# Gated linear attention and the choice of keys in one stage, the bias by distance made at x's load, norms inside the stages that take them

## What is computed

```python
def first_block(x, ...):
    h = rmsnorm(x, norm_g)                                   # n1
    p = h @ w_in                                             # split in gq, gk, gv, gz, ggate, dq, ... pu, pgate
    glog = log_sigmoid(gz @ gate_w2 + gate_b) / 16
    o_gla = rmsnorm(gla_mixer(gq, gk, gv, glog), gla_norm_g) # chunks of 64, state S carried, S = 0 at first
    y_gla = o_gla * silu(ggate)
    score = relu(q_idx . k_idx) weighed over 4 heads; idx = top_k(score, 128)    # the choice of keys
    o_dsa = softmax(q k^T * dh**-0.5 + rel_bias[bucket(t - s)]) v over the chosen keys
    y_dsa = o_dsa * silu(dgate)
    y_pool = ((windowed sums of pu) / count - pu) @ pool_w * pool_scale * silu(pgate)
    return rmsnorm(x + concat(y_gla, y_dsa, y_pool) @ w_out, final_norm_g)       # n2

def _layer_norm(x, gain, bias):                              # n3 to n8; n9 to n12 are rmsnorms
    xf = x - mean(x); return xf * rsqrt(mean(xf * xf) + 1e-5) * gain + bias
```

## Time and profile before

| | |
|---|---|
| three runs | 4337.07, 4345.38, 4340.18 us; median 4340.18 |
| the profiled execution | 4341.67 us, span 4339.9 us |
| TensorE busy, mean granted clock | 3704.6 us (85%), .903 |
| VectorE, ScalarE, GpSimd busy | 1404.9, 694.1, 228.7 us |
| gla stage, select stage, attend stage, pool stage | 299.2 to 418.8, 418.9 to 503.1, 503.2 to 643.7, 643.7 to 659.4 us |
| experts (bound by their loads) | 1476 to 2680 us |

### The profile page before, as it was taken

The page is one execution under the profiler, slowest core; times in us unless marked ns, Lnnn a source line. Parts: engine busy times, 40 slices in busy tenths (PEclk is TensorE's granted clock), DMA queues, the critical chain, the costliest instruction groups (busy, mean ns, idle before and its releaser), DMA issues. The chain is left out here.

```text
span 4339.9 us, 32097 instructions
## 1 busy us (share of the span) xinstructions
PE 3704.6 (85%) x11618; PEld 1792.0 (41%) x11618; DVE 1404.9 (32%) x2445; ACT 694.1 (16%) x1294; POOL 228.7 (5%) x241
## 2 busy tenths in 40 slices
PE   6985787899878499999999998694599767889998
PEld 2534343344343243434343443243344567434444
DVE  0005641177133221121211112427643489611011
ACT  1011120101111111010100000313243233110000
POOL 0000000300000100000000001000000345000000
PEclk8985578999999699999999998796799888999999
DMA  2210761722113599999999996111322000212120
GB/s 67 80 64 2 258 209 58 255 99 78 58 49 153 196 395 398 408 401 408 398 408 399 409 399 231 66 39 61 100 78 78 5 6 1 97 59 78 68 73 34
DMA packets 219295, 729.49 MB, mean 168 GB/s; under 512 B 16207, under 2 KB 27104, under 8 KB 184374
## 3 DMA queue, kind: packets, MB, share of 16 engines
q1 hardware_dynamic: 179132, 629.94, 38.4%
q10 hardware_dynamic: 28394, 55.66, 3.6%
q0 software_dynamic: 11664, 42.47, 2.8%
HBM read 678.33 MB, written 49.69 MB: 168 GB/s over the span
## 5 line engine op out<-in xcount | busy, mean ns | idle before, releaser
L1621 PE MATMUL bank<-moe_gu,all_hT 128*128 128x512 f32 x1088 | 472.1, 595 | 0.0
L1120 PE MATMUL bank<-all_hT,early_w 128*128 128x512 f32 x896 | 390.0, 598 | 22.6 <-PEq L135 11.7
L1811 DVE TENSOR_TENSOR all_hT<-bank,moe_bias 128x512 f32<-128x512 f32 x51 | 35.3, 691 | 973.6 <-PE bank L1621 683.3
L1621 PEld LDWEIGHTS bank<-moe_gu,all_hT 128*128 128x128 f32 x1088 | 207.6, 191 | 261.3 <-issue 261.3
L1647 PE MATMUL bank<-moe_dn,moe_rows 128*128 128x512 f32 x544 | 264.3, 648 | 46.2 <-DMA moe_dn<-in_w_dn_dram 45.3
L1120 PEld LDWEIGHTS bank<-all_hT,early_w 128*128 128x128 f32 x896 | 172.0, 192 | 240.7 <-issue 240.7
L1634 PE MATMUL bank<-moe_gu,all_hT 128*64 128x512 f32 x1088 | 236.5, 592 | 1.0 <-issue 1.0
L2334 PE MATMUL bank<-all_hT,hin_w 128*128 128x512 f32 x512 | 222.8, 598 | 13.1 <-DMA hin_w<-in_w_in_dram 13.1
L1120 PE MATMUL bank<-all_hT,late_w 128*128 128x512 f32 x512 | 222.8, 598 | 10.9 <-PEq L372 10.9
L1120 PE MATMUL bank<-b_up,late_w 128*128 128x512 f32 x512 | 220.0, 592 | 2.8 <-PEq L135 2.8
L2637 PE MATMUL bank<-hg_qs,hg_ks 128*128 128x128 f32 x896 | 143.3, 313 | 88.7 <-DVE hg_ks L2583 88.7
(11 more groups left out here) (541 smaller groups left out, 4113.7 us busy)
## 6 DMA issues: line engine op xcount, KB each, us to landing
moe_gu<-in_w_gu_dram SPq DMA_DIRECT2D x136, 2048.0 KB, 21.2
moe_dn<-in_w_dn_dram SPq DMA_DIRECT2D x68, 2048.0 KB, 22.9
early_w<-in_w_in_dram SPq DMA_DIRECT2D x13, 2048.0 KB, 9.2
expert_rows<-conv_zeros POOLq DMA_DIRECT2D x49, 512.0 KB, 17.2
early_w<-in_w_mod_dram SPq DMA_DIRECT2D x12, 2048.0 KB, 8.1
early_w<-in_ada_w_dram SPq DMA_DIRECT2D x12, 2048.0 KB, 8.0
hin_w<-in_w_in_dram SPq DMA_DIRECT2D x10, 2048.0 KB, 8.4
late_w<-in_w_up_dram SPq DMA_DIRECT2D x8, 2048.0 KB, 8.9
```

What stands on the lines that cost most here:

```text
L1120: mm = nc.tensor.matmul(B[b][:], w[:, k, m * P:(m + 1) * P], src[:, i * KT + k if stacked else k, :], start=(k == 0), stop=(k == KT - 1))
L1621: mm = nc.tensor.matmul(B[bank][:], xb2[:, k, :], gu[:, q, kk, col:col + HALF], start=(k == 0), stop=(k == KT - 1))
L1811: after(vec.tensor_tensor(g, gate[:], bias[0], ALU.add), 1)
```

## The change

- **`load_x`**: rel_bias times buckets, its two copies and the store to DRAM stand here now; SyncE issues their two loads ahead of x's.
- **`gla_and_select`** takes the place of `gla` and `dsa_select`. Score products, ReLU and weighing come first (12, block 0 has none), then the gates. Four of the twelve pieces of mod2 run beside the gates and exponentials, with a bank of their own, and eight after the norm's sums. VectorE's rounds are cut into steps of a generator: 11 before the decay, 2 behind it, 25 behind the masks, the rest at the end. The state that is zero is left out, and its four products with it. GpSimd issues the six bias windows and the flip matrix once TensorE has done the last product with the values, and waits for them.
- **`dsa_attend`** starts with the flips. `PoolMix` is a class: its sums advance one step after each unit's weights, its matmuls and scaling stand at the end, ahead of the gating. The pool stage is gone.
- **`Norm`** is a class with a part for each engine, emitted inside the block that takes its output; the consumer waits for each tile (`done`). Sums are made of fewer matmuls: for a mean 2 tiles alone and 3 sums of pairs (4 and 2 behind another norm), for squares 4 alone and 2 sums of pairs; VectorE adds the pairs. n1 is in `projection`, n2 and n3 in the mixer's first `linear`, n4 in the next, n6 and n7 in `route` (with its loads), n8 and n9 in `ssd_inputs`, n11 in the up-projection. n5 and n12 stay stages. n9's squares are made by VectorE, tile by tile as n8 is done. `finish_modulation` now stands ahead of n2, and it and `lower_bounds` ahead of n8.

```diff
 def load_x(core, a, xT, ident, ones):
...
+            sp.dma_start(rb[:], a["rel_bias"]).then_inc(table_loaded, 16)
+            sp.dma_start(onehot[:], core.const("bucket", BUCKETS)).then_inc(table_loaded, 16)
             sp.dma_start(ident[:], core.const("ident")).then_inc(loaded, 16)
...
+            sp.wait_ge(table_copied, 2)
+            sp.dma_start(a["bias_dram"], by_distance[:]).then_inc(stored, 16)
+            sp.wait_ge(stored, 16)
...
+class Norm:
...
+        self.alone = 2 if ready is None else 4
...
+    def sums(self, pe):
+        nc, ones = self.core.nc, self.ones
+        mean_ps, square_ps = self.core.bank[0], self.core.bank[1]
+        if self.centre:
+            for k in range(self.alone):
+                if self.ready is not None:
+                    pe.wait_ge(self.ready.done, k + 1)
+                nc.tensor.matmul(mean_ps[:], ones[:], self.src[:, k, :], start=(k == 0), stop=False)
+            for i, k in enumerate(range(self.alone, KT, 2)):
+                pe.wait_ge(self.paired, i + 1)
+                mm = nc.tensor.matmul(mean_ps[:], ones[:], self.scratch(k), start=False, stop=(k == KT - 2))
+            mm.then_inc(self.summed, 1)
+        for k in range(4):
+            pe.wait_ge(self.squared, k + 1)
+            nc.tensor.matmul(square_ps[:], ones[:], self.scratch(k), start=(k == 0), stop=False)
+        for i, k in enumerate((4, 6)):
+            pe.wait_ge(self.square_paired, i + 1)
+            mm = nc.tensor.matmul(square_ps[:], ones[:], self.scratch(k), start=False, stop=(k == 6))
+        mm.then_inc(self.square_summed, 1)
...
+    def vector(self, dve):
...
+            for k in range(self.alone, KT, 2):
...
+                nc.vector.tensor_tensor(scratch(k), self.src[:, k, :], self.src[:, k + 1, :],
+                                        ALU.add).then_inc(self.paired, 1)
...
+        for k in (4, 6):
+            dve.wait_ge(self.squared, k + 2)
+            nc.vector.tensor_tensor(scratch(k), scratch(k), scratch(k + 1), ALU.add).then_inc(self.square_paired, 1)
...
 def linear(core, stream, name, passes, src, evict, stacked=False, more=None, background=None, normed=()):
...
+            for n in normed:
+                n.sums(pe)
...
                         for k in range(KT):
+                            if normed and i + b == 0:
+                                normed[-1].wait(pe, k)
...
+def gla_and_select(core, to, ones, ident, gate_w2, gate_b, norm_g, y, spare, AT, pick, cond, mod, bias_dram, bias,
+                   flip, windows):
...
+            pool.wait_ge(pe_done, PE_NORM - GLA_H)
+            for h in range(DSA_H):
+                window = bass.AP(tensor=bias_dram.tensor, offset=h * 5 * P, ap=[[1, P], [1, T]])
+                pool.dma_start(bias(h), window).then_inc(windows, 16)
+            pool.dma_start(flip, core.const("flip")).then_inc(windows, 16)
+            pool.wait_ge(windows, 16 * (DSA_H + 1))
...
+            pe.wait_ge(relued, len(parts))
+            for c in range(EARLY_PIECES):
+                beside.multiply(pe, c)
+                beside.turn(pe, c)
             pe.wait_ge(dve_done, 4)
+            pe.wait_ge(beside.copied, EARLY_PIECES)
...
+            choose(11)
             dve.wait_ge(act_done, 7)
...
+            choose(2)
             dve.wait_ge(act_done, 9)
...
+            choose(25)
             dve.wait_ge(act_done, 18)
...
+            for _ in choice:
+                pass
...
 def dsa_attend(core, to, ident, ones, spare, bias, flip, windows, pick, y, cond, mod, pool_mix):
...
             pe.wait_ge(windows, 16 * (DSA_H + 1))
...
+                    next(sums, None)
+            pool_mix.scale(dve)
...
+            pe.wait_ge(peaked, N)
+            pool_mix.multiply(pe)
```

More of the change, by code:

```diff
@@ L361, in _ @@
             act.wait_ge(small, 64)
-def norm(core, name, src, dst, ones, scratch, gain, bias=None, centre=False, func=None, eps=EPS, loads=None):
+        @block.vector
+        def _(dve):
+            for i in range(2):
+                dve.wait_ge(table, i + 1)
+                cols = slice(0, 512) if i == 0 else slice(512, U)
+                nc.vector.tensor_copy(by_distance[:, cols],
+                                      core.bank[6 + i][0:DSA_H, 0:cols.stop - cols.start]).then_inc(table_copied, 1)
@@ L368, in norm @@
+def norm(core, name, src, dst, ones, scratch, gain, **more):
     nc = core.nc
-    plain = func is None and bias is None
-    func = func or ACT.Identity
-    mean_ps, square_ps = core.bank[0], core.bank[1]
     with ExitStack() as ctx:
[L373 to L376, removed]
+        alone = Norm(core, ctx, name, src, dst, ones, scratch, gain, **more)
@@ L377, in norm @@
         block = ctx.enter_context(nc.Block())
[L378 to L383, removed]
         @block.gpsimd
         def _(pool):
-            nc.gpsimd.memset(eps_col[:], eps).then_inc(eps_set, 1)
+            alone.clear(pool)
         @block.tensor
         def _(pe):
[L391 to L398, removed]
+            alone.sums(pe)
@@ L410, in _ @@
[L410 to L417 removed]
+            alone.vector(dve)
@@ L430, in _ @@
-            if not plain:
-                for k in range(KT):
-                    act.wait_ge(normed, k + 1)
-                    nc.scalar.activation(dst[:, k, :], scratch[:, k, :], func, scale=gain[:, k:k + 1],
-                                         bias=0.0 if bias is None else bias[:, k:k + 1]).then_inc(done, 1)
+            alone.scalar(act)
 OFF = {}
@@ L844, in _ @@
+            pe.wait_ge(windows, 16 * (DSA_H + 1))
+            for h in range(DSA_H):
+                nc.tensor.matmul(B[2 + h][:], flip, bias(h), start=True, stop=True).then_inc(flipped, 1)
             pe.wait_ge(flip_copied, DSA_H)
@@ L1355, in route, with _ @@
         block = ctx.enter_context(nc.Block())
+        @block.sync
+        def _(sp):
+            loads(sp)
         @block.gpsimd
         def _(pool):
+            for n in normed:
+                n.clear(pool)
             pool.wait_ge(copied, 8)
@@ L1415, in _ @@
         def _(dve):
+            for n in normed:
+                n.vector(dve)
             steps = Count(step)
@@ L2912, in square @@
                     nc.vector.tensor_tensor(up[:, n, :], up[:, n, :], up[:, n, :], ALU.mult).then_inc(squared, 1)
-            linear(core, late, "up", 4, hT, ("scalar", emit), more=square)
+            with ExitStack() as n:
+                n11 = Norm(core, n, "n11", xT, hT, ones, up[:, 3 * KT:, :], c["gain2"], mod[:, 24:32])
+                linear(core, late, "up", 4, hT, ("scalar", emit), more=square, normed=(n11,))
             linear(core, late, "down", 4, up, add_gated(40), stacked=True)
```

583 lines of the change are left out of this document (327 added, 256 removed).

## The result

The changed kernel takes 4184.14 us in the median of four runs (4179.79 to 4191.18), against 4338.62 for the kernel before (4335.05 to 4345.38). The ratio is 0.9638, with a 95% interval of 0.9625 to 0.9650. The forecast was 4188, with a range of 4167 to 4212. A second comparison, later, gave 0.9626 (0.9609 to 0.9642); over all nine runs of the changed kernel the median is 4180.9, and they scatter from 4173 to 4191.

What follows compares the result with a forecast made beforehand. TensorE is busy 85%, its granted clock sagging in seams and small matmuls. Norms -74.7, merged stage -49.7, attention -17.1, pool -10.9, +.3 and +.5 sum to -151.6: 4188 us against the median, range 4167 to 4212.

Steps and rivals of the forecast that it cites:

- (d): Rival in the linear layers: TensorE, fed tile by tile, starts and stays at 1.2 GHz; 4517 if one stage does; chance .01.
- Norms: Seams of the eleven norms: fewer ones-matmuls and overlap with neighbours save 74.7 us in total, bounds 61 to 79.
- Step (1): Norms' sums: pair additions on VectorE replace ones-matmuls; a mean saves 2.6 us warm, some 3.4 cold, squares 1.1 or 1.7.
- Step (2): Behind a norm: the consumer starts on tile 0, about 5.6 us after the last square, not 11.7; saves 6.1 at most.
- step (3): Where a norm follows a norm: the second's mean starts under the first's last pass; saves 7.4 us at n3, 6.9 at n7.
- The terms of n8 and n9: One chain from n8's mean to the next linear layer: 56.0 us becomes 40.2, saving 15.8, with a cold mean of 6.4.
- The merged stage: Gla and choice of keys in one stage: 204.0 us becomes 154.3, saving 49.7, with VectorE ending before TensorE, 8 to spare.
- the mean of the twelve: Late modulation pieces on TensorE in the merged stage: eight at 6.21 us each, the earlier average, 49.7 together.
- Rival (a): In the merged stage VectorE becomes the bound, TensorE's late pieces run at 2.4 GHz, end 8 us earlier: 4177; chance .17.
- The start: Beginning of the attention stage: with the bias table moved out, the flips come at once, saving 17.1 us.
- My +.5 for the additions: Attention loop: pool's additions fit VectorE's gaps in the first eleven units; cost 0 to +5 us, taken as +.5.
- x's load: Start of the kernel: the bias table placed there hides under the vectors' small transfers; up to +1 us, taken as +.3.

## Why the prediction was right

**The bound and the place of the gain.** Seams were where the time went, and every seam of the sum is there. The times of the long linear layers changed by less than 1 us each: (d), TensorE staying at 1.2 GHz, did not come.

**Norms.** Forecast 74.7, measured 70.8. Of the latter 1.2 is `mix_out`'s, whose first eight MATMUL rows took 5.37 us against 6.61, and .8 that of the layer ahead of n4, so the norms themselves gave some 69. Step (1), pairs, is right in size at n4. Step (2), the consumer behind tile 0, is right to .2 us (5.83 against "about 5.6"; 5.04 for n1). Where it was short is mainly step (3), a norm behind a norm: 1.0 at n7's mean, with .6 more at the router's products behind it, and 2.6 at n8 and n9. The terms of n8 and n9 were mis-sized by TensorE's clock: I let n9's squares end as fast as VectorE brought them, with a last matmul of 1.0, but after 9.71 us of idleness six matmuls took 7.8. n8's cold mean took 7.3 and not 6.4. The norms as stages showed the same: the overlap is worth 38, not 45.

**The merged stage.** Forecast 49.7 saved, measured 58.8, and the run with two stages confirms it (60). Of the 9: 1.7 is the early part (t = 43.7, not 45.4), 4.0 lies between the transposes and the end of the norm's sums (2.2 of it in the products L719, 4.28 us against 5.36, and the sums, 5.54 against 6.63), and 3.1 in the late pieces. The last of these is the mis-sized term of which I wrote that I take the mean of the twelve, as the same code under the same VectorE load gave it.

The trace shows where it went wrong: the first late piece took 4.0 us, with its products at 2.4 GHz (1.92 us against 3.64 before), the second 5.5, and the other six 6.2 each, as before. What ran ahead differed. The granted clock rose to 2.4 GHz at 390.5, while the sums ran, and stayed there until 397.3, with TensorE at work. Before the change it rose at 399.4, at the sums' end, and fell again at 402.8 with TensorE idle; after 18.9 us of idleness, 16 short products and 4.8 us more, the first four pieces took 6.55 each. All eleven traces with the merged stage have a first piece of 4.0, and both with two stages have four of 6.55 at the start. The lighter load of VectorE isn't the cause: in the run without early pieces VectorE has nothing to do in the last 29 us, and the pieces there still take 5.4 to 6.55 us.

```profile
431.60:460.40 28.80, 23.92 (x116) 10.93 (x108) 0.00 (x0) 3.57 (x9) 0.00 (x0) 0.56 0.95 336
```

VectorE's rounds didn't run to the end of the stage before, as I had read the earlier trace rows; they ended at 492.2, 11 us ahead of it. Rival (a) had the right sign (TensorE's clock a little higher) and the wrong end: VectorE came within 4.7 us and did not bound the stage. Taking the choice out of the gap made it the bound at once, for 21 us.

**Attention.** The start was right (16.7 against 17.1). The loop's -7.1 in the table can't be credited to the change. Its code is the same in all eleven traces with the merged stage but for the additions in one, and it took 106.1 us in six of them (.86), 108.8 in two (.83), and 109.8, 113.6 and 116.5 in one each (.81, .79, .77). The changed kernel itself gave 106.1 and 113.6. The two traces with two stages have 113.2 and 112.8; whether the merge makes the short loop more likely isn't shown. My +.5 for the additions holds: the kernel before and the changed kernel's second trace have the same granted clock, and the loop with 8 us more of VectorE's work took .4 longer.

```profile
529.35:642.55 113.20, 101.37 (x516) 49.65 (x516) 50.86 (x146) 31.13 (x95) 0.00 (x0) 0.79 0.60 201
```

**x's load** cost 1.2 and not .3, above the +1 that I had allowed. The two loads ahead of x's move its load by .9, but ScalarE's copies of x end only .1 later (22.0). The other 1.1 lies in the wait behind them, before the norm: 7.8 us against 6.75, and 6.4 in the run with the table back in the attention. In that wait the last small loads land and, new, the store of the bias table; which of them ends it isn't shown. These are the store's issue and TensorE's next work:

```profile
11.70 5.06 SPq L332 DMA_DIRECT2D bias_by_distance<-lx_by_distance  x1
...
31.90 5.47 PE L436 MATMUL bank<-b_y_rest,all_ones 128*128 128x512 f32 x8 [13.08 <-ACT b_y_rest L485]
...
44.13 6.09 PE L614 MATMUL bank<-all_hT,early_w 128*48 128x512 f32 x8 [5.04 <-DVE all_hT L470]
```

**Table load and windows.** A table load is 1.28 us in the trace after as well, with the next ACTIVATE .01 behind it at L769 (315.92 + 1.28, then 317.21), so the drain of the Trainium skill ("ScalarE: Activation LUTs", What ACT_TABLE_LOAD costs) has no sign here. The load that moved, at L775, has its ACTIVATE .24 behind it, and that waited for VectorE:

```profile
324.61 1.28 ACT L775 ACT_TABLE_LOAD   x1
326.13 1.91 ACT L775 ACTIVATE gla_e<-gla_lsig 48x2048 f32<-48x2048 f32 x1 [0.24 <-DVE gla_lsig L845]
```

The windows that GpSimd issues landed about as fast as they did from SyncE, where the median was 4.0:

```profile
b_gk<-bias_by_distance POOLq DMA_DIRECT2D x4, 256.0 KB, 3.8
b_gq<-bias_by_distance POOLq DMA_DIRECT2D x2, 256.0 KB, 4.5
```

But VectorE was idle while they were issued, in its 8.71 us before the reciprocal at 393.04, so that the warning of the Trainium skill ("SBUF — State Buffer", SBUF: two separate sides) was not put to the test.

**What came out even.** The two traces differ by 160.9 us, 9.3 more than the sum. 7.6 of that are the loop's, and 3.3 in the other direction are the third block's; both vary between executions. In the third block it is the stage of the mixers, in code that wasn't touched: from the last input product (`hin_w`) to the next `late_w` product it took 319.3 us before, 323.0 in the first trace of the changed kernel, 319.3 in the second, and 332.1 with the norms as stages. Without these two the sum was 5 us short: 9 more in the merged stage against 4 less in the norms. The medians differ by 154.5, 3 more than forecast. So the place and the mechanism of the gain were right, and that the total was only 4 us off is in part luck, since errors of both signs met. (4341.67 - 151.6 - 1.5 is 4188.6, so the forecast was rounded down.)

## What to carry to other kernels

Put a norm into the stage that takes it and let the consumer wait tile by tile: about 5 us each here, more than the smaller sums gave. Where two stages are bound by different engines, merging them pays by the shorter one's idle time, if the filler is cut into steps that fit the gaps; but leave the engine with the filler a margin, since with 26.7 us of steps put off it cost 21. And a short wait on a load in front of a chain of TensorE products can cost more than its length, when the products behind it then run at the lower clock: 3.47 us cost 7.4 and 6.6 in two traces. Load small operands a stage ahead.

## What was not expected of the hardware

The attention loop of one and the same program took 106.1 us in one execution and 113.6 in another, in step with the granted clock (.86 and .79), with no change in what the other engines do; over the eleven traces with the merged stage it ran from 106.1 to 116.5. In a stage of short products and short waits a difference of up to 7 us between two traces is therefore no finding. And twelve pieces of the same code took 70.7 us where they started at 2.4 GHz and 74.5 where they started at 1.2. The granted clock at their start was 2.4 GHz in each trace where they followed TensorE's work directly, and 1.2 in both where 18.9 us of idleness and 16 short products stood ahead.
